# Key and query lengths of a delta rule taken two stages earlier, their squares in another buffer, and four decay matmuls in the middle of a product

## The reference

```python
xn = _rms(x, norm_gain)                       # 512 x 1024
proj = xn @ w_in
qkv_a = silu(_causal_dwconv(proj[..., :A_QKV1], conv_w))      # 3 x 512 columns, 4 taps
q_a = _l2n(q part, 4 heads of 128); k_a = _l2n(k part); v_a = v part
z_a = proj[..., A_QKV1:A_Z1]                  # the delta rule's gate
beta = sigmoid(proj[..., A_Z1:A_B1])
g = -exp(a_log) * softplus(proj[..., A_B1:A_A1] + dt_bias)
o_a = _gated_delta_rule(q_a, k_a, v_a, g, beta)   # chunks of 64; uses q*dk**-0.5 and cumsum(g)
o_a = _rms(o_a, dn_out_gain) * silu(z_a)
... stick-breaking attention on q_b, k_b, v_b, its output times silu(z_b) ...

def _l2n(x):
    return x * lax.rsqrt(jnp.sum(x * x, axis=-1, keepdims=True) + EPS)
```

## Time and profile before

| | us |
|---|---|
| median of 3 runs | 1771.48 (1768.0 to 1773.71) |
| the profiled execution | 1772.76 |
| its span | 1770.7 |
| PE busy | 1523.5 (86% of the span) |
| PE weight loads | 1147.0 (65%) |
| DVE busy | 948.3 (54%) |
| ACT busy | 714.9 (40%) |
| POOL busy | 68.2 (4%) |

### The profile page before, as it was taken

The page is one execution under the profiler, slowest core; times in us unless marked ns, Lnnn a source line. Parts: engine busy times, 40 slices in busy tenths (PEclk is TensorE's granted clock), DMA queues, the critical chain, the costliest instruction groups (busy, mean ns, idle before and its releaser), DMA issues.

```text
span 1770.7 us, 17596 instructions
## 1 busy us (share of the span) xinstructions
PE 1523.5 (86%) x7159; PEld 1147.0 (65%) x7159; DVE 948.3 (54%) x1301; ACT 714.9 (40%) x1043; POOL 68.2 (4%) x80
## 2 busy tenths in 40 slices
PE   5999997798786963899999991989697899999999
PEld 4888775586565842555555551868585877678887
DVE  3444246623763445788888874675545535321334
ACT  4333334424443220666666662244322215652231
POOL 1000000000000000111011101000000000000000
PEclk9999998998997986899999996999897988999999
DMA  6422221122104430999999984220101003002241
GB/s 197 168 96 75 96 73 66 68 75 72 70 26 161 152 119 23 307 327 340 331 336 335 329 294 156 72 71 26 47 1 48 1 24 119 1 1 72 95 143 48
DMA packets 80348, 224.01 MB, mean 127 GB/s; under 512 B 9044, under 2 KB 10182, under 8 KB 76167
## 3 DMA queue, kind: packets, MB, share of 16 engines
q1 hardware_dynamic: 71558, 193.73, 32.3%
q0 software_dynamic: 6144, 20.71, 3.5%
q10 hardware_dynamic: 2560, 8.39, 1.3%
HBM read 200.00 MB, written 22.81 MB: 126 GB/s over the span
## 4 chain that ended last, share of the span: by engine, by line
PE 59%; DVE 25%; ACT 11%; DMA 2%; issue 2%; SPq 1%; POOL 0%; DVEq 0%; POOLq 0%; ACTq 0%
PE PS L502 14%; PE PS L504 14%; PE PS L503 14%; DVE wlo L1152 7%; DVE htlo L1152 5%; PE PS L928 4%; ACT whi L1950 3%; PE PS L499 3%; DVE ylo L1152 2%; ACT work L1950 2%; PE PS L1077 2%; ACT yhi L1950 2%; PE PS L1068 1%; ACT hthi L1950 1%; DVE work L1561 1%
## 5 line engine op out<-in xcount | busy, mean ns | idle before, releaser
L1152 DVE TENSOR_TENSOR wlo<-raw,whi 128x2048 fp32r<-128x2048 f32 x74 | 169.1, 2291 | 356.3 <-ACT whi L1950 356.3
L1950 ACT ACTIVATE whi<-raw 128x2048 fp32r<-128x2048 f32 x74 | 141.2, 1912 | 334.9 <-PE PS L504 333.5
L499 PE MATMUL PS<-consts,work 128*128 128x128 f32 (+1 forms) x652 | 100.7, 298 | 125.9 <-DVE work L1178 53.2
L502 PE MATMUL PS<-whi,hthi 128*128 128x512 f32 x480 | 200.1, 417 | 9.2 <-ACT work L1950 6.4
L502 PE MATMUL PS<-hthi,whi 128*128 128x512 f32 x480 | 198.3, 413 | 5.1 <-ACT scratch L1950 2.8
L503 PE MATMUL PS<-wlo,hthi 128*128 128x512 f32 x480 | 190.9, 398 | 0.0
L504 PE MATMUL PS<-whi,htlo 128*128 128x512 f32 x480 | 190.8, 398 | 0.0
L504 PE MATMUL PS<-hthi,wlo 128*128 128x512 f32 x480 | 190.0, 396 | 0.0
L503 PE MATMUL PS<-htlo,whi 128*128 128x512 f32 x480 | 189.5, 395 | 0.0
L499 PEld LDWEIGHTS PS<-consts,work 128*128 128x128 f32 (+1 forms) x652 | 85.2, 182 | 155.1 <-DVE work L1178 54.4
L1950 ACT ACTIVATE work<-PS 128x512 f32<-128x512 f32 (+3 forms) x204 | 103.3, 531 | 88.6 <-PE PS L992 51.2
(11 more groups left out here) (320 smaller groups left out, 2600.3 us busy)
## 6 DMA issues: line engine op xcount, KB each, us to landing
raw<-in_w_in SPq DMA_DIRECT2D x44, 1024.0 KB
raw<-in_w SPq DMA_DIRECT2D x80, 512.0 KB
scratch<-in_w SPq DMA_DIRECT2D x48, 512.0 KB
raw<-in_w SPq DMA_DIRECT2D x19, 1024.0 KB
scratch<-in_w SPq DMA_DIRECT2D x13, 1024.0 KB
raw<-in_w_gate SPq DMA_DIRECT2D x8, 1024.0 KB
raw<-in_w_out SPq DMA_DIRECT2D x8, 1024.0 KB
y_scratch<-work ACTq DMA_DIRECT2D x32, 256.0 KB, 7.1
```

The costliest lines, as they stand in the source:

```text
L499: return e.transpose(o, i, ident[0:n, 0:n])
L502: e.matmul(o, lh, rh, start=start, stop=False)
L1152: tt(lo, raw_place(j), as_f32(hi), SUB).then_inc(*ve.mark("lo", j))
L1950: return e.activation(o, i, f, bias=bias, scale=scale)
```

## The change

In the change a function `length(n)` in both programs takes one length. The query's (0) stands ahead of the third block of convolutions: on ACT between `to_natural(1)`'s copies and the copies of the third `qa` product, on DVE between that block's splits and its convolutions. The key's (1) stands ahead of the gate `za`. The squares go to `LSQ`, a view on the idle `y_plain`. PE's four decay matmuls are issued when `zb` is through its first unit, DVE's copy of them and ACT's exponentials ahead of the gate `zb`. No arithmetic is added or left out.

```diff
+    LSQ = y_plain[:, 0, 0:HB, :].rearrange("p k n -> p (k n)")
-        def product(name, b, turned, hi, lo, ready=None, by_k=None):
+        def product(name, b, turned, hi, lo, ready=None, by_k=None, halfway=None):
...
+                if kh == 0 and halfway:
+                    halfway()
...
-        product("zb", 0, True, hthi, htlo, h_ready)
-        ps = fresh("sums")
...
+        def decay_sums():
+            ps = fresh("sums")
...
+        product("zb", 0, True, hthi, htlo, h_ready, halfway=decay_sums)
# vector
+        def length(n):
+            part, tag = NAT[:, :, n * NH:(n + 1) * NH], f"len{n}"
+            on.wait_ge(*ac["squares", tag])
+            red(stat[tag][0], LSQ.rearrange("p (g d) -> p g d", d=DK), ADD).then_inc(*ve.mark("length", n))
+            settle()
+            r = inverse_rms(tag, N16, 1.0)
+            if n == 0:
+                settle()
+                ts(r, r, DK ** -0.5, None, MUL).then_inc(*ve.mark())
+            settle()
+            for i in range(NT):
+                v4 = heads(part[:, i, :])
+                tt(v4, v4, bc(by_tile(r, i), [P, DH, DK]), MUL).then_inc(*ve.mark())
         for blk in range(3):
             split()
             split()
             if blk == 0:
                 split()
+            if blk == 2:
+                length(0)
...
         e.tensor_copy(dta, inside("dta")[:, 0:2 * DH]).then_inc(*ve.mark("out", "dta"))
+        length(1)
         silu_gate("za", ZA)
         split()
...
-        for n in range(2):
-            part, tag = NAT[:, :, n * NH:(n + 1) * NH], f"len{n}"
...
         ve.also("lengths")
         split()
+        on.wait_ge(*pe["sums"])
+        e.tensor_copy(sums, inside("sums")[:, 0:4 * N16]).then_inc(*ve.mark("out", "sums"))
+        settle()
+        tt(edl, sums[:, N16:2 * N16], gc, SUB).then_inc(*ve.mark("edl"))
         silu_gate("zb", ZB)
         e.memset(S, 0.0).then_inc(*ve.mark("state0"))
         ve.also("tiles clear")
-        on.wait_ge(*pe["sums"])
...
         split()
# scalar
+        def length(n):
+            if n:
+                on.wait_ge(*ve["length", 0])
+            settle()
+            act(tiles(LSQ), NAT[:, :, n * NH:(n + 1) * NH], ACT.Square).then_inc(*ac.mark("squares", f"len{n}"))
+            root(f"len{n}", N16)
...
             if blk:
                 to_natural(blk - 1)
+            if blk == 2:
+                length(0)
...
+        length(1)
         silu_gate("za", lambda c: ve["silu", 10 + c])
...
         split()
-        silu_gate("zb", lambda c: ve["out", "za", 0, HB - 2 + c])
-        ac.also("tiles clear")
         on.wait_ge(*ve["edl"])
         act(edl, edl, ACT.Exp).then_inc(*ac.mark())
         act(gend, sums[:, 2 * N16:], ACT.Exp).then_inc(*ac.mark())
         act(egc, gc, ACT.Exp).then_inc(*ac.mark("decays"))
+        silu_gate("zb", lambda c: ve["out", "za", 0, HB - 2 + c])
+        ac.also("tiles clear")
         split()
```

More of the change, by code:

```diff
@@ L902, in tensor @@
         to_natural(2)
-        product("zb", 0, True, hthi, htlo, h_ready)
-        ps = fresh("sums")
[L905 to L916, removed]
+        def decay_sums():
+            ps = fresh("sums")
+            on.wait_ge(*ve["gl"])
+            on.wait_ge(*ve["masks"])
+            e.matmul(ps[:, 0:N16], causal, gflat, start=True, stop=True)
+            e.matmul(ps[:, N16:2 * N16], same, gflat, start=True, stop=True).then_inc(*pe.mark())
+            for c in range(2):
+                r_ = slice(64 * c, 64 * c + 64)
+                on.wait_ge(*pe.now())
+                m = e.matmul(ps[:, (2 + c) * N16:(3 + c) * N16], ones[r_, :], gflat[r_, :], start=True, stop=True)
+                if c == 0:
+                    m.then_inc(*pe.mark())
+            m.then_inc(*pe.mark("sums"))
+            bank.filled(("sums",))
+        product("zb", 0, True, hthi, htlo, h_ready, halfway=decay_sums)
         def turn4(i, name, src):
@@ L1703, in vector @@
         stt(gl, gl, -1.0, ea.unsqueeze(1).broadcast_to([P, NT, DH]), MUL, MUL).then_inc(*ve.mark("gl"))
-        for n in range(2):
-            part, tag = NAT[:, :, n * NH:(n + 1) * NH], f"len{n}"
[L1708 to L1718, removed]
         ve.also("lengths")
         split()
-        silu_gate("zb", ZB)
-        e.memset(S, 0.0).then_inc(*ve.mark("state0"))
-        ve.also("tiles clear")
         on.wait_ge(*pe["sums"])
@@ L1727, in vector @@
         tt(edl, sums[:, N16:2 * N16], gc, SUB).then_inc(*ve.mark("edl"))
+        silu_gate("zb", ZB)
+        e.memset(S, 0.0).then_inc(*ve.mark("state0"))
+        ve.also("tiles clear")
         split()
```

## The result

The changed kernel took 1779.61 us (median of 7 runs, 1776.0 to 1783.1), the kernel before 1772.29 (1768.0 to 1773.71) beside it: a ratio of 1.0048 with a 95% interval of [1.0031, 1.0065]. Forecast were 1773.1 us and a range that ended at 1779. The profiled execution took 1777.37 us, its span is 1775.4.

What follows compares the result with a forecast made beforehand. PE was taken to bound the time ahead of the delta tiles, then a chain of DVE, PE and ACT latencies. 6.7 - 4.7 + 0.6 - 1.0 = +1.6 us gave a median of about 1773.1 us, range 1767 to 1779.

Steps and rivals of the forecast that it cites:

- Part 1: Query's length ahead of ACT's copies of the third `qa` product: 6.3 us added ahead of `ba`, `za` +6.7 us on PE.
- Part 2: Key's length ahead of the gate `za`: `zb` starts 0.25 us later, on top of the 6.7.
- Part 3: Decay sums in the middle of `zb`: their 1.34 us of PE moved, not added, with 1.4 us of slack.
- Part 4: From `zb` to the delta tiles: late load hidden, DVE's first delta instruction -4.7 us, before the 6.7 is added.
- The clock at `ba`: Matmuls of `ba` at half clock after PE's 9 us idling: between 0 and 3.3 us, taken as +0.6.
- The clock at the delta tiles: Less half clock at the delta tiles after PE's shorter wait there: taken as -1.0 us.
- another 7%: Later stage: its stretches at half clock may fall otherwise once everything is shifted, some us either way; 7%.
- (a): Rival: the stall at `ba` doesn't come, so the kernel takes 1765.8 us; 12%.
- (b): Rival: clock stays low after the 9 us stall, through `ba` into `za`, and at the delta tiles: +6.5 us, 1778; 13%.
- (c): Rival: each of four new table switches on parts 1 and 2 costs a 1.38 us drain: +5.5 more, 1778.6; 3%.

Runs made afterwards that it cites:

- before_act_busy: The kernel before with three more squares of 128x2048 on ACT ahead of its copies of the third `qa` product; ratio 1.0051 to the kernel before.
- q_between: The change with the query's length moved between the third block's two splits, the key's as in the change; ratio 0.9976 to the kernel before.
- lengths_alone: The change with the decay sums back behind `zb`, their copy and exponentials back behind the gate; ratio 1.0042 to the kernel before.
- two_copies_first: The change with ACT's first two copies of the third `qa` product ahead of the query's length; ratio 1.0035 to the kernel before.
- after_again: The changed kernel, unedited, timed a second time; ratio 1.0027 to the kernel before.
- after_third: The changed kernel, unedited, timed a third time; ratio 1.0014 to the kernel before.
- both_in_gaps: q_between with the key's length also moved, from ahead of the gate `za` to behind the third block's convolutions; ratio 0.9976 to the kernel before.

## Why the prediction was wrong

The mechanics came out as worked; the clock did not.

- **Part 1**, right. Predicted 6.3 us at `ba` and 6.7 at `za`; in the frame of the copies to `NAT`, 1186.66 + 2.2 - 1182.60 = 6.3 and 1194.83 + 2.2 - 1190.16 = 6.9. PE's idle time of "about 9 us" is 8.99. before_act_busy and q_between show it from both sides.
- **Part 2**, right: `zb` at 1218.99 + 2.2 = 1221.2, 6.96 later than the earlier trace rows; predicted 6.7 + 0.25.
- **Part 3**, right: PE has no wait at the sums.
- **Part 4**, right: predicted 2.0 us later for DVE's first delta instruction (6.7 - 4.7), measured 2.2; the load left the chain, and PE's wait fell to 3.3 against about 3. That no table load stands on the chain there holds too. q_between, without part 1's stall, has the tiles 4.5 earlier: the -4.7.
- **The clock at `ba`**, right in its way, too large in size: nine matmuls ran at half clock, where before had some seven, which took 0.3 us more (0.6 in the other two profiles). Of the +0.6 that was added to the 6.7, only 0.2 reached `za`, which had to wait for its bank anyway.
- **The clock at the delta tiles**: the -1.0 came as -1.1 in the pair of profiles compared, but by luck. Against the other two profiles of before nothing is won there. Nor does it last. Over the 40 us from where the half clock sets in, the granted clock was 0.79, 0.83 and 0.83 in the profiles of before and 0.79, 0.83 and 0.83 in those of the change, so the half clock that the shorter wait saves at the first products comes back within the next ones:

```profile
1243.00:1283.00 40.00, 26.01 (x141) 21.07 (x141) 22.47 (x32) 11.08 (x18) 0.00 (x0) 0.79 0.08 27
1248.00:1288.00 40.00, 30.99 (x167) 26.13 (x168) 22.29 (x35) 9.50 (x15) 0.00 (x0) 0.79 0.08 27
```

- **The failed step** is the sum's treatment of the clock in the stage behind the tiles' first 10 us: it stood at nothing, and was put into "another 7%" and "by some us either way", while the -1.0 ahead of it was counted as if it would last. In the profile compared, that stage came as +5.6 us (2.4 and 3.2), more than the net of all moves (2.2). Over the three comparisons the change costs 5.8 us, about 2 either way, of which the place of the tiles is 2.2 to 2.4; the forecast was +1.6, and the first medians gave +7.3. The range, 1767 to 1779, had taken the run-to-run scatter of the clock for smaller than it is: three runs of before had shown 1768.0 to 1773.71, while 35 runs on one other chip spread from 1770.97 to 1785.04.

Of the rivals, (a) is false: the stall came. (b) had the size of the first comparison (+6.5 against +7.3) for a wrong reason: the half clock ended in `ba` after nine of 24 matmuls and reached nothing of `za` (granted 1.00 from 1192). (c) is false: the load at 1184.37 takes 1.28 and the root behind it starts at 1185.66, 1.29 later. The Trainium skill, page "ScalarE: Activation LUTs", section "What ACT_TABLE_LOAD costs", adds a drain of 1.38 to each switch; no row here has it.

**What stays open** is how much of the rest is the stall's. By the last column of the table, the kernels with a stall of 7.7 to 9.0 us around `ba` (the change, before_act_busy, lengths_alone, two_copies_first) lost 3.4, 2.7, 3.4 and 0.7 us beyond the move of their tiles, 2.6 on average; the seven without it +2.6 to -2.6, +0.1 on average. The granted clocks of all executions point the same way. Time at half clock, worked out as twice the span times what the mean clock lacks to 1, was 0.5 to 14.7 us more than in before beside it for the kernels with the stall (7.6 on average, after_again and after_third counted singly), and for the seven others +3.5 to -7.4 (-1.6 on average). That points to some 2 to 3 us that a long stall costs later, through the clock. But most values of the column have 3.5 us either way, kernels that were timed together share the runs of before, before against itself had 6.4 and 2.4 us less at half clock, and the profiles place the half clock differently each time: it is suggested, not shown. The place alone, 2.2 to 2.4 us, is some two fifths of the 5.8.

**A better version** is q_between, or both_in_gaps. It keeps what the change was worth (4.5 us at the tiles) and pays nothing for it, since the length lies in ACT's wait for PE. That it beats the change is clear (0.994). That it beats the kernel before is likely: 0.9976 [0.9958, 0.9993], some 4 us, but from one comparison, where before against itself gave 0.9986 and 0.9993. The profile of q_between doesn't settle it: of the 4.8 us at the tiles, 0.2 is left at the last matmul against the first profile of before, the rest having gone in stretches at half clock.

## What to carry to other kernels

Ahead of an engine's in-order work, ask of a moved step not whether the engine has time for it, but what stands behind it and who waits for that: six microseconds ahead of two copies stopped TensorE for as many, while the same step one split earlier, inside a wait for TensorE, cost nothing. Where a move shortens a later wait, it repays only that wait: here 4.7 of 6.7 us. On a kernel whose clock falls and rises between stages, put the scatter of the clock into the range from the start; here three comparisons of one edit gave 1.0048, 1.0027 and 1.0014. And when two profiles are compared, look first at a stretch ahead of the edit: 1.4 us of "later" stood there in two of the three profiles of the change.

## What the runs showed of the hardware

The time of an unchanged kernel spreads by 0.8%, and its granted clock goes with it: 35 runs of before on one chip went from 1770.97 us (clock 0.924 in that run) to 1785.04 (0.916), and the longer runs have the lower mean clock. Over the runs of one kernel, a microsecond more at half clock (by the mean clock) went with 0.22 to 0.45 us more time. The two levels are 1.2 and 2.4 GHz, and which matmuls run at the lower one differs between executions: the same sixteen transposes took 1.95, 2.28, 2.72 and 3.62 us. Two profiles therefore differ by several microseconds in stages that an edit does not touch, and the edit's part is better read from the times of many runs.
